# A second low-rank stage in split rounded products with eight staging tiles

## The reference

```python
xx = token_shift(x) - x
xr, xw, xk, xv, xa, xg = (x + xx * mu[i] for i in range(6))
r, k, v = xr @ w_rkv[0], xk @ w_rkv[1], xv @ w_rkv[2]
w_log = -softplus(-(w0 + tanh(xw @ w1) @ w2)) - 0.5       # w1 1024x64, w2 64x1024
a = sigmoid(a0 + (xa @ a1) @ a2)                          # a1 1024x64, a2 64x1024
g = sigmoid(xg @ g1) @ g2                                 # g1 1024x160, g2 160x1024
```

## Time and profile before

| | |
|---|---|
| median of 3 executions | 1371.79 us (1368.88 to 1372.1) |
| the profiled execution | 1370.31 us, of which 1368.6 us span |
| TensorE busy | 1310.5 us, 96% |
| mean granted TensorE clock | 0.975 |

### The profile page before, as it was taken

The page is one execution under the profiler, slowest core; times in us unless marked ns, Lnnn a source line. Parts: engine busy times, 40 slices in busy tenths (PEclk is TensorE's granted clock), DMA queues, the critical chain, the costliest instruction groups (busy, mean ns, idle before and its releaser), DMA issues.

```text
span 1368.6 us, 23052 instructions
## 1 busy us (share of the span) xinstructions
PE 1310.5 (96%) x9193; PEld 1072.0 (78%) x9193; DVE 667.1 (49%) x891; ACT 511.3 (37%) x885; POOL 578.4 (42%) x355
## 2 busy tenths in 40 slices
PE   7999999999999998999997999999999999999996
PEld 6888788888888883377775888888888888888885
DVE  2486821112344468146457788774671111344447
ACT  4453232232223222434343677675233222323230
POOL 4344344443544450225434455546045444444440
PEclk9999999999999998999997999996999999999998
DMA  7234243332544312534523112012334333333321
GB/s 277 77 93 124 65 135 93 92 104 64 170 121 120 96 62 77 210 121 145 167 95 124 33 49 78 20 33 94 108 93 123 92 95 104 93 98 102 92 61 61
DMA packets 113423, 139.01 MB, mean 102 GB/s; under 512 B 10386, under 2 KB 86210, under 8 KB 113348
## 3 DMA queue, kind: packets, MB, share of 16 engines
q1 hardware_dynamic: 108740, 121.16, 29.4%
q10 hardware_dynamic: 4608, 16.78, 3.2%
HBM read 123.24 MB, written 14.68 MB: 101 GB/s over the span
## 4 chain that ended last, share of the span: by engine, by line
PE 78%; DVE 13%; issue 3%; ACT 3%; DMA 2%; SPq 1%; POOL 1%; ACTq 0%; DVEq 0%; POOLq 0%
PE bank L1543 35%; PE bank L1628 9%; PE bank L1630 9%; PE bank L1629 9%; DVE a_lo L1077 2%; PE bank L1809 2%; PE bank L1723 2%; DVE x_tok L1107 2%; DVE x_tok L1109 2%; DVE stats L1096 2%; DVE x_tok L1129 1%; PE bank L1850 1%; DMA proj<-stage 1%; PE bank L1734 1%; PE bank L1973 1%
## 5 line engine op out<-in xcount | busy, mean ns | idle before, releaser
L439 POOL TENSOR_TENSOR w_lo<-raw,w_hi 128x1024 fp32r<-128x1024 f32 x176 | 432.5, 2462 | 625.2 <-ACT w_hi L633 582.9
L633 ACT ACTIVATE w_hi<-raw 128x1024 fp32r<-128x1024 f32 x176 | 184.2, 1055 | 279.3 <-PE bank L1543 267.2
L1543 PE MATMUL bank<-w_hi,a_hi 128*128 128x512 f32 x760 | 236.3, 392 | 6.2 <-DVE a_lo L1077 5.6
L1628 PE MATMUL bank<-xT_hi,w_hi 128*128 128x512 f32 (+1 forms) x640 | 236.3, 369 | 3.9 <-POOL w_lo L439 3.9
L1629 PE MATMUL bank<-xT_lo,w_hi 128*128 128x512 f32 (+1 forms) x640 | 235.4, 368 | 0.0
L1630 PE MATMUL bank<-xT_hi,w_lo 128*128 128x512 f32 (+1 forms) x640 | 235.4, 368 | 0.0
L1543 PE MATMUL bank<-w_lo,a_hi 128*128 128x512 f32 x760 | 234.3, 389 | 0.0
L1543 PE MATMUL bank<-w_hi,a_lo 128*128 128x512 f32 x760 | 234.2, 389 | 0.0
L1077 DVE TENSOR_TENSOR a_lo<-big,a_hi 128x512 fp32r<-128x512 f32 x64 | 140.7, 2204 | 182.5 <-ACT a_hi L652 179.4
L1194 DVE TENSOR_TENSOR big<-relu 128x512 f32 (+1 forms) x64 | 45.8, 716 | 274.0 <-ACT relu L758 274.0
L1543 PEld LDWEIGHTS bank<-w_hi,a_hi 128*128 128x128 f32 x760 | 140.7, 188 | 41.6 <-issue 12.2
(11 more groups left out here) (262 smaller groups left out, 1679.6 us busy)
## 6 DMA issues: line engine op xcount, KB each, us to landing
raw<-in_ffn_w SPq DMA_DIRECT2D x128, 512.0 KB, 3.9
raw<-in_rw_w_rkv SPq DMA_DIRECT2D x24, 512.0 KB, 3.8
proj<-stage ACTq DMA_DIRECT2D x24, 512.0 KB, 2.6
raw<-in_gm_w_in SPq DMA_DIRECT2D x16, 512.0 KB, 4.0
early<-proj SPq DMA_DIRECT2D x8, 1024.0 KB, 6.1
raw<-in_gm_w_out SPq DMA_DIRECT2D x8, 512.0 KB, 3.6
raw<-in_rw_w_o SPq DMA_DIRECT2D x8, 512.0 KB, 3.5
late<-proj SPq DMA_DIRECT2D x8, 512.0 KB, 3.9
```

The source lines that it names most:

```text
L439: nc.gpsimd.tensor_tensor(w_lo[:, j, :], raw[:, j, :], w_hi[:, j, :].bitcast(F32), ALU.subtract).then_inc(w_lo_ready, 1)
L633: nc.scalar.activation(w_hi[:, j, :], raw[:, j, :], ACT.Copy).then_inc(w_hi_ready, 1)
L1543: last = nc.tensor.matmul(bank[2 * t + h][:], a[:, j, tok], w[:, h * HALF:(h + 1) * HALF], start=start and m == 0, stop=stop and m == 2)
L1628: nc.tensor.matmul(dst, w_hi[:, j, col], xT_hi[:, k, tokens], start=k == 0, stop=False)
```

## The change

- The second stage of w and a is done as split rounded products. The weights of both stand in one tile `wa2`, w in rows 0 to 63 and a in rows 64 to 127, and so do the left operands (`low_wa`). Each half tile is four rounded matmuls of 64 rows: hi hi, hi lo, the bias, lo hi. Matmuls of w and a alternate, in two row halves and two banks.
- The bias is a rounded product as well: a constant `share` of 1/32 against `bias_parts`, whose rows are 32 times the rounded bias and 32 times the rest of it. ACT rounds it, DVE subtracts.
- The 128-row part of g is three rounded matmuls; the 32-row part stays in full precision.
- The weights are split by DVE in the last but one group of down0; the left operands by ACT and DVE between the two stages. w's Tanh is done twice, once rounded. w and a no longer wait for g's first stage (`wa_summed`).
- The order is w/a of token tile 0, g of tiles 0 and 1, w/a of 1 and 2, g of 2 and 3, w/a of 3. DVE evicts g (`drain_g`), ACT w and a (`drain_wa`); ACT issues all stores, from eight staging tiles.
- k_k, k_a and r_k are loaded after the first four receptance slabs, because the new left operands lie in their place. The small loads of down0 are in another order.

```diff
+        WA_STAGE = ((0, 1), (4, 5), (6, 7), (2, 3))
+        G_STAGE = (2, 3, 0, 1)
+        WA_BANK, G_BANK = (0, 0, 4, 4), (4, 6, 0, 2)
 ...
@@ SyncE
                         if (name, i) == ("key", 0):
                             sp.wait_ge(slab_used, first_slab["key"])
+                            for half, vector in ((W_ROWS, rw_w0), (A_ROWS, rw_a0)):
+                                sp.dma_start(bias[half, :], vector.partition_broadcast(LORA).rearrange("p a n -> p (a n)")
+                                             ).then_inc(bias_in, 16)
 ...
+                        if (name, i) == ("receptance", 0):
+                            sp.wait_ge(slab_used, first_slab["key"] + 1)
                             for row, vector in ((k_k, rw_k_k), (k_a, rw_k_a),
 ...
@@ ScalarE
+            act.wait_ge(bias_in, 32)
+            nc.scalar.activation(bias_parts[:], bias[:], ACT.Copy).then_inc(bias_rounded, 1)
+            act.wait_ge(wa_summed, 1)
+            nc.scalar.activation(low_wa_hi[W_ROWS, :], bank[4][W_ROWS, :], ACT.Tanh).then_inc(low_ready, 1)
+            nc.scalar.activation(low_wa[W_ROWS, :], bank[4][W_ROWS, :], ACT.Tanh).then_inc(low_ready, 1)
             act.wait_ge(lora_summed, 1)
-            nc.scalar.activation(low_w[0:LORA, :], bank[4][0:LORA, :], ACT.Tanh).then_inc(low_ready, 1)
-            nc.scalar.activation(low_a[0:LORA, :], bank[5][P - LORA:P, :], ACT.Copy).then_inc(low_ready, 1)
             nc.scalar.activation(low_g[:], bank[6][:], ACT.Sigmoid).then_inc(low_ready, 1)
             nc.scalar.activation(low_gb[:], bank[7][:], ACT.Sigmoid).then_inc(low_ready, 1)
 ...
+            def drain_wa(t):
+                for b in WA_STAGE[t]:
+                    if t == TT - 1:
+                        act.wait_ge(low_out[b], 16)
+                for h in range(2):
+                    for side, summed in enumerate((bank_projected, a_projected)):
+                        b = WA_STAGE[t][side]
+                        act.wait_ge(summed, 2 * t + h + 1)
+                        nc.scalar.activation(low_stage[b][:, h * HALF:(h + 1) * HALF], bank[WA_BANK[t] + 2 * side + h][:],
+                                             ACT.Sigmoid).then_inc(proj_read, 1)
+                for side, which in enumerate((SIG, AA)):
+                    act.wait_ge(proj_read, 4 * t + 3 + side)
+                    store_low(which, t, WA_STAGE[t][side])
+            def store_g(t):
+                act.wait_ge(g_read, 2 * t + 2)
+                store_low(4 + GG, t, G_STAGE[t])
 ...
-            for u, function in enumerate((ACT.Sigmoid, ACT.Sigmoid, ACT.Copy)):
-                for t in range(TT):
-                    act.wait_ge(bank_projected, TT * u + t + 1)
-                    projected(u, t, function)
+            drain_wa(0)
+            store_g(0)
+            drain_wa(1)
+            store_g(1)
+            drain_wa(2)
+            drain_wa(3)
+            store_g(2)
+            store_g(3)
@@ VectorE, in down0
+                dve.wait_ge(wa_in, 48)
+                for j in range(SLOTS):
+                    low(last - 1, j)
+                    split_low_weights(j)
@@ VectorE, after the first low-rank stage
+            nc.vector.memset(share[:].bitcast(F32), 1.0 / Q).then_inc(ones_ready, 1)
+            dve.wait_ge(bias_rounded, 1)
+            for m in (1, 3):
+                nc.vector.tensor_tensor(bias_parts[quadrant(m), :], bias[quadrant(m), :],
+                                        bias_parts[quadrant(m), :].bitcast(F32), ALU.subtract).then_inc(ones_ready, 1)
+            dve.wait_ge(wa_summed, 1)
+            nc.vector.tensor_copy(low_wa_hi[A_ROWS, :], bank[5][A_ROWS, :]).then_inc(low_split, 1)
 ...
+            dve.wait_ge(low_ready, 3)
+            nc.vector.tensor_copy(low_g_hi[:], low_g[:]).then_inc(low_split, 1)
+            dve.wait_ge(low_split, 4)
+            nc.vector.tensor_tensor(low_g_lo[:], low_g[:], low_g_hi[:].bitcast(F32), ALU.subtract).then_inc(low_split, 1)
+            def drain_g(t):
+                b = G_STAGE[t]
+                if t >= 2:
+                    dve.wait_ge(low_out[b], 16)
+                for h in range(2):
+                    dve.wait_ge(g_projected, t + 1)
+                    nc.vector.tensor_copy(low_stage[b][:, h * HALF:(h + 1) * HALF], bank[G_BANK[t] + h][:]).then_inc(g_read, 1)
 ...
                     if k + 2 < KT:
                         mix_slab(k + 2)
+                    if u == 0 and k < 2:
+                        drain_g(k)
+                    if u == 0 and k == 1:
+                        drain_g(2)
+                        drain_g(3)
@@ TensorE
+            def project_wa(t):
+                if t == 0:
+                    pe.wait_ge(wa_split, 2)
+                    pe.wait_ge(low_ready, 1)
+                    pe.wait_ge(low_split, 1)
+                    pe.wait_ge(ones_ready, 3)
+                elif t == 1:
+                    pe.wait_ge(proj_read, 4)
+                elif t == 2:
+                    pe.wait_ge(g_read, 4)
+                else:
+                    pe.wait_ge(proj_read, 12)
+                tok = slice(t * P, (t + 1) * P)
+                for h in range(2):
+                    col = slice(h * HALF, (h + 1) * HALF)
+                    for m, (a, w) in enumerate(((low_wa_hi[:, tok], wa2_hi), (low_wa_hi[:, tok], wa2_lo),
+                                                (share, bias_parts), (low_wa_lo[:, tok], wa2_hi))):
+                        if (t, h, m) == (0, 0, 3):
+                            pe.wait_ge(low_split, 3)
+                        for side, (rows, summed) in enumerate(((W_ROWS, bank_projected), (A_ROWS, a_projected))):
+                            last = nc.tensor.matmul(bank[WA_BANK[t] + 2 * side + h][:], a[rows, :], w[rows, col],
+                                                    start=m == 0, stop=m == 3)
+                            if m == 3:
+                                last.then_inc(summed, 1)
+            def project_g(t):
+                if t == 0:
+                    pe.wait_ge(wa_split, 4)
+                    pe.wait_ge(low_ready, 4)
+                    pe.wait_ge(low_split, 5)
+                else:
+                    pe.wait_ge(proj_read, 8)
 ...
+            project_wa(0)
+            project_g(0)
+            project_wa(1)
+            project_wa(2)
+            project_g(2)
+            project_wa(3)
 ...
+            def low_rank_read(t):
+                if t < 2:
+                    pe.wait_ge(g_read, 4 + 2 * t + 2)
+                else:
+                    pe.wait_ge(proj_read, 4 * TT)
```

More of the change, by code:

```diff
@@ L172, in trunk @@
         lg1b = over("lg1b", [P, KT, COPIES, REST])
-        lw2 = over("lw2", [LORA + 1, D])
-        la2 = over("la2", [LORA + 1, D])
+        wa2 = over("wa2", [P, D])
+        wa2_hi = over("wa2_hi", [P, D], F32R)
         lg2 = over("lg2", [P, D])
+        lg2_hi = over("lg2_hi", [P, D], F32R)
         lg2b = over("lg2b", [P, D])
[L177 to L181, removed]
+        wa2_lo = sb("wa2_lo", [P, D], F32R, at=place["wa2"])
+        lg2_lo = sb("lg2_lo", [P, D], F32R, at=place["lg2"])
+        assert cursor[0] <= place["big"] and 2 * LORA == P
+        W_ROWS, A_ROWS = slice(0, LORA), slice(LORA, P)
+        bias_parts = over("bias_parts", [P, D], F32R)
         xxT = over("xxT", [P, KT, S])
@@ L185, in trunk @@
         stage = over("stage", [P, 2, D])
+        cursor[:] = place["k_k"], place["gains"]
+        low_wa = over("low_wa", [P, S])
+        low_wa_hi = over("low_wa_hi", [P, S], F32R)
+        low_g = over("low_g", [P, S])
+        low_g_hi = over("low_g_hi", [P, S], F32R)
+        low_gb = over("low_gb", [P, S])
+        share = over("share", [P, P], F32R)
+        bias = over("bias", [P, D])
+        low_wa_lo = sb("low_wa_lo", [P, S], F32R, at=place["low_wa"])
+        low_g_lo = sb("low_g_lo", [P, S], F32R, at=place["low_g"])
+        low_stage = [*(sb(f"low_stage{b}", [P, D], at=place["lw1"] + 4 * D * b) for b in range(3)),
+                     *(sb(f"low_stage{3 + b}", [P, D], at=place["lora_mix"] + 4 * D * b) for b in range(3)),
+                     stage[:, 0, :], stage[:, 1, :]]
         cursor[:] = place["xT_hi"], place["k_k"]
@@ L1208, in mlp, with split_low_weights @@
                     low(0, j)
-                with dve.Fori(1, last + 1) as i:
+                if layer:
+                    with dve.Fori(1, last + 1) as i:
+                        for j in range(SLOTS):
+                            low(i, j)
+                    return
+                with dve.Fori(1, last - 1) as i:
                     for j in range(SLOTS):
                         low(i, j)
+                dve.wait_ge(wa_in, 48)
+                for j in range(SLOTS):
+                    low(last - 1, j)
+                    split_low_weights(j)
+                for j in range(SLOTS):
+                    low(last, j)
+            def split_low_weights(j):
+                raw2, hi, lo = ((wa2, wa2_hi, wa2_lo), (lg2, lg2_hi, lg2_lo))[j // 2]
```

(19 more changed lines are left out.)

95 lines of the change are left out of this document (43 added, 52 removed).

## The result

| | before | after |
|---|---|---|
| median | 1369.72 us (10 runs, 1361.46 to 1372.1) | 1354.64 us (10 runs, 1350.47 to 1358.76) |
| the profiled execution | 1370.31, span 1368.6 | 1354.58, span 1352.5 |
| ratio after / before | | 0.9901, 95% interval 0.9880 to 0.9922 |

The forecast was 1362.0 us with a range of 1358.5 to 1367.5. One later execution of the kernel before took 1380.58 us at a mean clock of 0.966; it is left out of all that follows. The page of the changed kernel, to be read beside the earlier trace rows: TensorE has 13 us less work, and landings of stores, 2% of the chain before, stand at 0%.

A forecast was written before the change was run, and what follows sets the result against it. TensorE, busy 96% of the span, was taken as the bound. Slab 0 ending at 576.4, not 585.5, gains 9.1 us: 1361.2 from the profiled execution, 1362.7 from the median; 1362 was taken, range 1358.5 to 1367.5.

The forecast's parts named there:

- stops for the split: First w/a block: TensorE does three pairs, then waits for VectorE's subtractions until 551.95.
- the idle: Before the third w/a block: TensorE waits 2.5 us, 559.1 to 561.6, released by VectorE's eviction of g tile 1.
- the last drain: ScalarE's last four evictions, before the key product: from 569.9, done by 572.1, wanted at 573.4, so no delay.
- a w/a block: Second stage: 8 pairs of row halves side by side at 0.227 us each, 1.82 us a block.
- a g block: Second stage: 2.72 us of rounded products plus 1.14 us of 32-row full-precision ones, 3.86 us.
- a change of height: Between second-stage blocks: taken to cost nothing seen; seven changes, estimated at about 1.1 us less gain, stayed out of the sum.
- An idle of 2.5 us is on the side of the first: 1.6 us: Behind the new TensorE idle: clock falls as after an earlier 1.97 us idle, losing 1.6 us, zero the other bound.
- The lower time of the two bases and 1 us of error: Low end of the range for the whole kernel: that base and error, with no clock loss, give 1358.5 us.
- (a): Second-stage w/a blocks: row halves run in turn, adding 1.6 + 1.8 + 1.8 us; gain 3.9, time 1366.4; chance 0.09.
- The parts that cost nothing: Outside the second stage: moved weight splits, bias rounding, bias and row-gain loads, and later a_lo and w_lo add no time.
- (b): VectorE's g tile 1 evictions held by GpSimd: up to 3.6 us more, 1364.9; chance 0.12, shared with other new waits.
- (c): Last drain waits for stores landing one by one at 5.75 us: kernel 8.7 us slower, 1379; chance 0.05.

The follow-up runs named there:

- again_after: The changed kernel run once more, nothing edited: stage 51.2 us, median 1356.38 us, ratio 0.9925 to the kernel before.
- filler: The changed kernel with 43 rounded 128x512 matmuls, not used in any result, put before the key product: stage 60.9 us, median 1367.00 us, ratio 0.9990 to before.
- again_before: The kernel before the change run once more against itself: stage 61.5 us, median 1367.08 us, ratio 1.0002.
- full_all: The changed kernel with only the rounding undone (w, a and g's 128-row part in full precision): stage 53.3 us, median 1362.44 us, ratio 0.9960 to before.
- halves_in_turn: The changed kernel with w's four terms issued ahead of a's four, not alternating: stage 52.4 us, median 1360.81 us, ratio 0.9963 to before.
- act_evicts_g: The changed kernel with g evicted by ScalarE, nothing by VectorE, blocks reordered: stage 54.4 us, median 1359.85 us, ratio 0.9938 to before.
- same_half: The changed kernel with w's and a's matmuls both in the upper row half: stage 60.5 us, median 1368.12 us, ratio 1.0012 to before.

## Why the prediction was right and wrong

**The mechanism, right.** By its own steps, with 1.16 us added for the later start: TensorE starts on w and a at 552.16 (552.07 measured), stops for the split by 0.25 us (0.28), the idle is 2.5 us (2.26) and has the named releaser, the last drain starts when TensorE lets it. The key product started at 571.16; forecast, without a clock loss, 569.1 + 1.16 = 570.3. Of the missing 0.9 us, 0.3 lie ahead of the idle's end. The other 0.6 lie where the height changes: a w/a block took 2.04 us from its start to the next work, not 1.82, and a g block 4.04, not 3.86. The prediction put a change of height at nothing, by a start against a modelled end. The starts of the kernel before showed 0.1 us already: 572.36 to 572.88 is 0.52 us, where full-precision records of this block stand 0.43 apart. The 1.1 us that the prediction left out of its sum would have been nearer. Slab 0 took another 0.2 us more than forecast.

**The first step that failed: the clock behind the new idle.** "An idle of 2.5 us is on the side of the first: 1.6 us". It was sized by the length of the idle, from the earlier trace rows. The idle of 2.26 us here, in again_after and in filler left the clock at 1.00; one of 2.23 us in again_before, and one of 1.97 us in the profile before, were followed by 0.50. Those of 1.92 us in full_all and 2.13 us in halves_in_turn left it at 1.00 as well. The changed kernel (length, PE busy, granted clock, DMA share, GB/s) and, under it, again_before (its window with PEld, DVE, ACT and POOL behind PE):

```profile
558.00:564.00 6.00, 3.74 (x32) 1.00 0.55 221
564.00:570.00 6.00, 6.00 (x40) 1.00 1.01 348
```

```profile
569.02 6.78 PE L1734 MATMUL bank<-lg,low_g 128*128 128x512 f32 x8 [2.23 <-ACT stage L791]
...
570.00:572.00 2.00, 2.00 (x4) 0.93 (x3) 0.00 (x0) 1.09 (x2) 0.00 (x0) 0.50 0.67 272
```

Ahead of the two with a fall stood 32 records of 65 rows, one after the other. Ahead of the other five stood row halves side by side. act_evicts_g shows a fall at 3.09 us without serial half-height matmuls, same_half one at 0.45 us with them. That the height decided in the kernel before too is argued from this, not shown: no run changed the height, the idle or its moment in that kernel. Its loss, half of 3.4 us in one profile and of 6.8 us in the other, is in what the change took away. With that term at zero the sum gives a stage of 50.1 us (51.1 and 51.2 measured) and a gain of 10.7 us (9.7 to 10.3). The 1.6 us of the clock that did not come and the 1.0 us by which the stage was longer otherwise work against each other. That 9.1 us came out near the stage's measured gain is partly luck.

**The second step that failed, and the larger: the base and the range.** "The lower time of the two bases and 1 us of error" was the wrong step for the range. The base came from three executions that lay high: 1371.8 and 1370.3, where the 109 have a mean of 1367.4. And these 109 differ by up to 14.6 us. Their times follow their clocks. In the profile before, 44.4 us between 700 and 1000 us ran at 1.2 GHz, in again_before 34.1; half of the difference is 5.1 us of work. A gain of 9.1 us from 1367.4 would have been 1358.3, with at least 4 us to either side. The forecast time was 7.4 us too high: 4.4 by the base (1371.8 against 1367.4, of which the choice of 1362 in place of 1362.7 took back 0.7), 2.8 by the gain (9.1 against 11.9 between the means; the stage holds 0.6 to 1.2 of these 2.8, the rest lies outside it and stays open), and 0.9 by the draw of the ten runs (1354.64 against 1355.5). The high end was summed wrong too: (a) on the higher base is 1371.8 - 3.9 = 1367.9, not 1367.5.

**The parts that cost nothing** cost nothing: from key slab 5 to the up product the means of two profiles differ by 3.8 us, the two profiles of the kernel before by 4.8. Rival (a) did not occur, but same_half shows its price: with the clock it would have taken the whole gain, not 5.2 us of it. (b) did not occur: 1.28 us for two evictions beside GpSimd. (c) did not occur with eight tiles; with two it did.

**Which part is worth what**, read from the stage: 61.1 us before (mean of two), 56.5 with the staging alone and no clock loss, 53.3 with row halves side by side as well, 51.2 with rounded products as well. Rounding without the row halves: 55.0. So the staging, with the order of blocks and VectorE's evictions that go with it, is 4.6 us; without the before kernel's own clock loss, 2.6 us by the mean of two profiles, it is about 2. The row halves are 3.1 to 3.8 us, the rounding 1.5 to 2.1. The kernel with the staging alone also leaves the bias out, so its 56.5 us is of slightly different work.

## What to carry to other kernels

Buy side by side before you buy cheaper: putting two products of half height into the two row halves gave more than splitting them into rounded terms, and it kept TensorE's clock up. When TensorE's clock is part of the sum, read what stood ahead of its fall, height of the matmuls included, and not only how long the engine was idle. And before a base is taken from a few executions, ask how far the same kernel's clock differs from one to the next: here the times of the same kernel spread over more than the effect.

## What the runs showed of the hardware that was not expected

- 64-row matmuls in one row half, one after the other, were followed by 10.2 us at 1.2 GHz in two kernels, in one profile of each, although TensorE was idle for only 0.45 and 0.67 us. The same at 128 rows stayed at 2.4 GHz, in one profile of each. Without an idle they were not seen to lower the clock.
- Matmuls of different row halves started together (557.708 and 557.721 us) although, as worked out above, three others stood between them in the program; where a wait stood between them they did not.
- A change of height in the sequence of matmuls cost about 0.1 us: 0.33 us between starts in place of 0.23.
- One kernel's time goes by 1.1 us for each 0.001 of mean granted clock; over 109 executions the clock ran from 0.972 to 0.984.
